# The first pair's turned rows made by TensorE products in a two-layer hybrid decoder with a mixture of experts

## What is computed

```python
def hier_moe(h, w_rg, b_rg, w_re, b_re, w_gate, w_up, w_down):
    xf = h.reshape(n_tok, d)                      # 512 tokens, d = 1024; h = rmsnorm(x)
    g_top = jnp.argmax(xf @ w_rg + b_rg)          # 1 of 4 groups
    chosen = (xf @ w_re + b_re)[of that group]    # 8 experts in it
    top_vals, top_idx = lax.top_k(chosen, 2)      # 2 experts a token
    weights = p_g[:, None] * jax.nn.softmax(top_vals, axis=-1)
    ...                                           # rows of a token are sent to its experts
    y = (jax.nn.silu(xc @ w_gate[e]) * (xc @ w_up[e])) @ w_down[e]
    ...                                           # weighted sum over a token's two experts
```

## Time and profile before

| what | value |
|---|---|
| median of three runs | 1655.12 us |
| profiled execution | 1655.6 us, of which the span is 1653.9 us |
| TensorE busy | 1560.3 us (94% of the span) |
| VectorE, ScalarE, GpSimd busy | 715.5, 308.2, 46.8 us |
| mean granted TensorE clock | 0.972 |
| DMA | 458 MB, mean 277 GB/s |

### The profile page before, as it was taken

The page is one execution under the profiler, slowest core; times in us unless marked ns, Lnnn a source line. Parts: engine busy times, 40 slices in busy tenths (PEclk is TensorE's granted clock), DMA queues, the critical chain, the costliest instruction groups (busy, mean ns, idle before and its releaser), DMA issues. The chain is left out here.

```text
span 1653.9 us, 19530 instructions
## 1 busy us (share of the span) xinstructions
PE 1560.3 (94%) x7428; PEld 730.9 (44%) x7428; DVE 715.5 (43%) x1550; ACT 308.2 (19%) x640; POOL 46.8 (3%) x62
## 2 busy tenths in 40 slices
PE   8999996999999999989999999997799999999995
PEld 4444452444443444445654444554344444444442
DVE  3222344334343333347265389824333333333335
ACT  2000120100000000022244277822000000000002
POOL 0000000000000000000000000000000000000000
PEclk9999997999999999999899899999899999999998
DMA  6271409999999999955210300072899999999993
GB/s 204 77 266 64 169 26 344 420 421 419 421 420 420 421 421 420 421 199 164 77 55 23 153 2 1 1 271 82 345 421 420 420 420 421 421 420 421 420 420 149
DMA packets 111931, 458.03 MB, mean 277 GB/s; under 512 B 29520, under 2 KB 56144, under 8 KB 62672
## 3 DMA queue, kind: packets, MB, share of 16 engines
q1 hardware_dynamic: 106352, 448.23, 67.5%
q0 software_dynamic: 5472, 8.40, 1.4%
HBM read 461.83 MB, written 6.29 MB: 283 GB/s over the span
## 5 line engine op out<-in xcount | busy, mean ns | idle before, releaser
L968 PE MATMUL ps<-raw,e_xT 128*64 128x512 f32 x2112 | 474.4, 600 | 16.8 <-DMA raw<-in_expert_w_up 16.8
L968 PEld LDWEIGHTS ps<-raw,e_xT 128*64 128x64 f32 x2112 | 154.7, 138 | 322.8 <-issue 321.5
L1105 DVE TENSOR_TENSOR e_sg_hid<-e_sg_hid,ps 64x512 f32<-64x512 f32 x66 | 45.0, 681 | 410.3 <-ACT e_sg_hid L1046 410.0
L1091 DVE TENSOR_TENSOR x_res<-x_res,ps 128x512 f32<-128x512 f32 x272 | 173.9, 681 | 4.3 <-PE ps L1006 2.1
L411 PE MATMUL ps<-c_hT,raw 128*128 128x512 f32 x384 | 165.2, 592 | 0.1
L996 PE MATMUL ps<-raw,e_hT 128*64 128x512 f32 x704 | 163.5, 607 | 1.3
L1054 ACT ACTIVATE e_yhi<-ps,e_wtab 128x512 fp32r<-128x512 f32 x66 | 45.3, 687 | 415.3 <-PE ps L996 415.3
L1046 ACT ACTIVATE e_sg_hid<-ps 64x512 f32<-64x512 f32 x66 | 39.2, 594 | 445.0 <-PE ps L968 445.0
L1777 PE MATMUL ps<-a_spare,raw 128*128 128x512 f32 x256 | 115.8, 609 | 3.8 <-DVE a_spare L1538 3.8
L1006 PE MATMUL ps<-e_yhi,e_pick 64*128 64x512 f32 x528 | 112.0, 421 | 6.5 <-DVE x_res L1091 4.8
L1084 DVE SCALAR_TENSOR_TENSOR e_ylo<-ps,e_wtab,e_yhi 128x512 fp32r<-128x512 f32 x66 | 49.6, 751 | 149.3 <-ACT e_yhi L1054 149.3
(11 more groups left out here) (289 smaller groups left out, 1357.7 us busy)
## 6 DMA issues: line engine op xcount, KB each, us to landing
raw<-in_expert_w_gate SPq DMA_DIRECT2D x128, 1024.0 KB, 25.6
raw<-in_expert_w_up SPq DMA_DIRECT2D x128, 1024.0 KB, 26.9
raw<-in_expert_w_down SPq DMA_DIRECT2D x88, 1024.0 KB, 27.0
e_raw<-in_expert_w_down SPq DMA_DIRECT2D x40, 1024.0 KB, 26.5
raw<-in_conv_w_in SPq DMA_DIRECT2D x11, 1024.0 KB, 9.7
raw<-in_w_kv SPq DMA_DIRECT2D x6, 1024.0 KB, 6.3
raw<-in_conv_w_out SPq DMA_DIRECT2D x1, 4096.0 KB, 19.0
raw<-in_attn_w_in SPq DMA_DIRECT2D x4, 1024.0 KB, 5.3
```

The lines of the kernel that those rows point to most:

```text
L968: mm = pe.matmul(ps_gu[C - C * i:2 * C - C * i, :], xT[:, q % 2, k, u * C:(u + 1) * C], ring(m, L, p)[:, kk * F:(kk + 1) * F], start=(k == ...
L1091: return dve.tensor_tensor(x, x, bank[:], ALU.add).then_inc(done, 1)
```

## The change

The gather of the first pair is gone. Instead, TensorE forms the turned rows of experts 0 and 1 directly: `x` of a token tile, every eighth column (`m.x[:, t, k:D:NK]`), is the operand loaded as weights, and the one-hot `first`, now float32 and scaled with the token's inverse norm (`rstd`), is the moving operand. There are 4 tiles times 8 groups of features, 32 products of 128x128 by 128x128, summed over the tiles in PSUM banks 4 and 2.

- The products of tiles 0 to 2 (24 of 32) stand before the last tile's choice: three before the last logits, 21 behind them. For them `rank` of tile 2 is made inside the last quarter and signalled (`s_ahead`), and VectorE makes the one-hots of those tiles (`first_pair(range(NT - 1))`, seven operations) between the last tile's two quarter additions. The other 8 products follow the last rank.
- The one-hot of one tile is two `tensor_scalar` operations of 128x64 with two per-partition factors, where one `tensor_tensor` of 128x512 made all four.
- `slots` moves out of the router's block into the experts' block (`vector_slots`), behind the scaling of the first pair.
- The place list (`vector_table`, `tensor_places`) moves behind chunk 0's down products, the indices, `vector_tail` and the table of weights to chunk 1; the table of weights stands in the middle of chunk 1's gate and up products. The second pair is turned in chunk 1, both halves, instead of one in chunk 0 and one in chunk 1.
- Pieces 8 to 11 are issued ahead of the last tile's `rows_x`, pieces 16 and 17 at the start of the experts' block without a wait, and the two `kv_scale` loads go to the end of the convolution.
- `m.code`, `idx0` and their operations are gone; several small tiles now lie in `coded`.

The loop on SyncE with the wait for `s_wt` is not touched.

```diff
@@ sync_ring
         for t in range(NT):
+            if t == NT - 1:
+                sp.wait_ge(self.s_o, 2 * NT + 1)
+                prefetch(sp, self.m, self.L, range(8, 12))
             sp.wait_ge(self.s_xn, t + 1)
             sp.dma_start(self.m.rows_x[self.L][t * P:(t + 1) * P, :], self.xn[:, t % 2, :]).then_inc(self.s_out[t % 2], 16)
-        sp.wait_ge(self.s_o, 2 * NT + 1)
-        prefetch(sp, self.m, self.L, range(8, 11))
@@ Router.tensor
+        def taken(tiles, ks):
+
+            for k in ks:
+                for t in tiles:
+                    mm = pe.matmul(m.ps[(4, 2)[k // HK]][:, k % HK * GS:(k % HK + 1) * GS], m.x[:, t, k:D:NK],
+                                   self.first[:, t, :], start=(t == 0 and k % HK == 0),
+                                   stop=(t == NT - 1 and k % HK == HK - 1))
+            return mm
...
+                    if part == 1 and k == 5:
+                        rank(t - 1).then_inc(self.s_ahead, 1)
...
         logits(NT - 1, 1, 0)
         turn(NT - 1, 1, 1)
+        pe.wait_ge(self.s_near, NT - 1)
+        pe.wait_ge(self.s_ev[0], NT)
+        taken(range(NT - 1), range(1))
         logits(NT - 1, 1, 1)
+        taken(range(NT - 1), range(1, NK))
         rank(NT - 1)
...
-        pe.wait_ge(self.s_near, 1)
-        for t in range(NT):
-            for i in range(2):
-                mm = pe.matmul(m.ps[2][:, 0:1], self.first[:, t, :], m.code[:, i, t:t + 1],
-                               start=(t == 0 and i == 0), stop=(t == NT - 1 and i == 1))
-        mm.then_inc(self.s_found, 1)
+        pe.wait_ge(self.s_near, NT)
+        for h in range(2):
+            taken(range(NT - 1, NT), range(h * HK, (h + 1) * HK)).then_inc(self.s_taken, 1)
@@ first_rows
-        pool.wait_ge(self.s_idx0, 1)
-        for s in self.s_out:
-            pool.wait_ge(s, 16 * (NT // 2))
-        self.gather(pool, 0, self.idx0[:])
@@ Router.vector
+        def first_pair(tiles):
+
             rank = m.ps[7][:, 0:NT * E].rearrange("p (t e) -> p t e", t=NT)
+            part = slice(tiles[0], tiles[-1] + 1)
+            own.step(dve.scalar_tensor_tensor(out=self.near[:, part], in0=rank[:, part, 0:PAIR], scalar=1.0,
+                                              in1=self.both[:, part, 0:PAIR], op0=ALU.add, op1=ALU.mult))
+            for t in tiles:
+                for e in range(PAIR):
+                    c = dve.tensor_scalar(self.first[:, t, e * C:(e + 1) * C], m.iota[:, 1:C + 1], self.near[:, t, e:e + 1],
+                                          m.rstd[:, self.n, t:t + 1], ALU.is_equal, ALU.mult)
+                c.then_inc(self.s_near, 1)
...
                 for part in range(2):
                     add(t, 1, part)
                     moved(t, part)
+                    if part == 0:
+                        dve.wait_ge(self.s_ahead, 1)
+                        first_pair(range(NT - 1))
...
         choose(NT - 1)
-        first_pair()
-        slots()
+        dve.tensor_tensor(self.w[:, 0, :], self.top[:, 1, :], self.top[:, 0, :], ALU.subtract).then_inc(self.s_ge, 1)
+        dve.wait_ge(self.s_rank, 1)
+        first_pair(range(NT - 1, NT))
@@ experts
-                if c == 0 and b == 0:
-                    r.tensor_places(pe)
+                if c == 1 and b == 0:
+                    pe.wait_ge(r.s_cw, 1)
+                    r.tensor_table(pe, ps_c[0][0], r.rhot[:].bitcast(F32), r.cwts[:], 2).then_inc(s_wt, 1)
...
             pe_transpose(pe, c)
-            if c + PAIR < NCH:
-                pe_turn(pe, c + PAIR)
+            for n in turns(c):
+                pe_turn(pe, n)
...
             pe_down(pe, c)
+            if c == 0:
+                r.tensor_places(pe)
...
-            sp.wait_ge(r.s_rows[0], 16)
-            prefetch(sp, m, L, (11, *range(NR0, NR)))
...
+            prefetch(sp, m, L, range(NR0, NR))
...
-            own = r.vector_table(dve)
-            r.vector_indices(dve, own)
-            r.vector_tail(dve, own)
+            own = r.vector_slots(dve)
...
-            for n in range(PAIR):
-                pe_turn(pe, n)
             for c in range(NB):
                 pe_step(pe, c)
```

More of the change, by code:

```diff
@@ L320, in _ @@
             r.sync_weights(sp)
+            with nc.allow_non_contiguous_dma(reason="small vectors"):
+                sp.dma_start(m.kv_scale[:, 0, :], a["norm_kv"].rearrange("(k p) -> p k", p=P)).then_inc(m.kv_gain, 16)
+                sp.dma_start(m.kv_scale[:, 1, :], a["norm_mix"][1].rearrange("(k p) -> p k", p=P)).then_inc(m.kv_gain, 16)
             prefetch(sp, m, 0, (6, 7, 12, 13, 14, 15))
@@ L490, in __init__ @@
         self.coded = sb(keep, "coded", [P, NTK * (C + 3 * NCH)])
+        marks = self.coded[:, 0:NTK * C].rearrange("p (w t e) -> p w t e", w=4, t=NT)
+        self.oh, self.slot, self.late = marks[:, 0:2], marks[:, 2], marks[:, 3]
+        self.first = self.coded[:, NTK * C:NTK * C + NT * GS].rearrange("p (t s) -> p t s", t=NT)
+        small = self.coded[:, NTK * (C + 2 * NCH):NTK * (C + 2 * NCH) + 8 * E].rearrange("p (w e) -> p w e", w=8)
+        self.zero, self.prior, self.hot, self.sel, self.cap, self.chunk, self.ovn, self.begin = (small[:, i] for i in range(8))
+        self.shift = self.coded[:, NTK * (C + 2 * NCH) + 8 * E:NTK * (C + 2 * NCH) + 8 * E + 2]
         self.idx, self.tok = sb(keep, "idx", [P, NCH // PAIR], U32), sb(keep, "tok", [P, NCH])
-        self.idx0 = sb(keep, "idx0", [P, 1], U32)
         self.rows = sb(keep, "rows", [P, 2, D])
@@ L495, in __init__ @@
         self.far = sb(keep, "far", [P, NCH])
-        self.near, self.first = sb(tmp, "near", [P, NT, PAIR]), sb(tmp, "first", [P, NT, GS], BF16)
+        self.near = sb(tmp, "near", [P, NT, PAIR])
         self.both = sb(tmp, "both", [P, NT, E], BF16)
@@ L755, in scaled_weights @@
             dve.wait_ge(self.s_wg, 1)
-        def first_pair():
-            dve.tensor_tensor(self.w[:, 0, :], self.top[:, 1, :], self.top[:, 0, :], ALU.subtract).then_inc(self.s_ge, 1)
-            dve.wait_ge(self.s_rank, 1)
-            rank = m.ps[7][:, 0:NT * E].rearrange("p (t e) -> p t e", t=NT)[:, :, 0:PAIR]
-            own.step(dve.scalar_tensor_tensor(out=self.near[:], in0=rank, scalar=1.0, in1=self.both[:, :, 0:PAIR],
-                                              op0=ALU.add, op1=ALU.mult))
-            dve.tensor_tensor(self.first[:].rearrange("p t (e c) -> p t e c", e=PAIR),
-                              m.iota[:, 1:C + 1].unsqueeze(1).unsqueeze(1).broadcast_to([P, NT, PAIR, C]),
-                              self.near[:].unsqueeze(3).broadcast_to([P, NT, PAIR, C]), ALU.is_equal).then_inc(self.s_near, 1)
-            dve.wait_ge(self.s_found, 1)
-            dve.tensor_scalar(self.idx0[:], m.ps[2][:, 0:1], FAR, None, ALU.add).then_inc(self.s_idx0, 1)
@@ L1049, in act_step @@
                 act.wait_ge(s_wtab, 1)
+                for s in r.s_out:
+                    act.wait_ge(s, 16 * (NT // 2))
             if NY <= c < E:
@@ L1072, in dve_turned @@
             q, h = n // 2, n % 2
-            wait(dve, s_xt, n + 1)
+            if n < PAIR:
+                dve.wait_ge(r.s_taken, n + 1)
+            else:
+                dve.wait_ge(s_xt, n - 1)
             wait(dve, s_used, (2 * q - 4) * NPIECE + 2 * NPIECE)
@@ L1216, in _ @@
             pool.wait_ge(r.s_idx, 2)
+            for s in r.s_out:
+                pool.wait_ge(s, 16 * (NT // 2))
             r.gather(pool, 1)
```

151 lines of the change are left out of this document (72 added, 79 removed).

## The result

The changed kernel is slower: 1661.93 us, median of 6 runs (1659.36 to 1663.53), against 1653.93 us (6 runs, 1650.1 to 1655.31) for the kernel before, measured beside it. The ratio is 1.005, 95% interval 1.004 to 1.006. The profiled execution took 1663.53 us, with a span of 1661.7; before, it was 1655.6. The forecast was 1645.0, range 1641 to 1659. The measured time is outside it, and within 1 us of the first rival's 1662.7.

What follows compares the result with a forecast made beforehand. The prediction took both layers' expert stages to end with the DMA's stream of weight pieces; -12.5 us (layer 0) and +1.2 (layer 1) on the profiled 1655.6 gave 1644.3, rounded to 1645, range 1641 to 1659.

Steps and rivals of the forecast that it cites:

- first rival: New products' weight loads run at ScalarE's strided pace, 0.54 us a product: 1662.7 us, slower; chance 0.22.
- the price with no row: Cost of new products loading x with a step of 8 floats: 0.222 us each taken, 0.54 the upper bound.
- Stages end with the stream of pieces: Both layers' expert stages end when the DMA's stream of weight pieces, at 420 GB/s, ends.
- One-hots 1.4 us: Last quarter, layer 0: VectorE makes three tiles' one-hots, near and six operations, in 1.4 us to 243.1.
- Rank at 250.3 and first gate product at 254.65: Layer 0: last rank delayed by 0.2 us only, first gate product at 254.65 instead of 261.77, 7.1 us earlier.
- Stream of layer 0: Layer 0's unbroken stream of pieces begins at 260.4 instead of 273.0: 12.6 us earlier, taken as 12.5.
- Stream of layer 1: Layer 1's stream starts at s_wt, 18.4 us after the first gate product, at 1176.1: 1.2 us later than before.
- Full clock behind the router: Behind the router TensorE's granted clock is 1.0 (2.4 GHz), where the mean was 0.76 from 260 to 280 us.
- Two chunks in 29 us: Experts' stage: chunks 0 and 1 take 29 us from first gate product, so layer 0's chunk 2 starts at 283.7.
- The second: Rival: weight loads about twice as long, 0.37 to 0.45 us a product, +8.6 to +13.2, 1653 to 1657.5; chance 0.18.
- The third: Rival: clock 0.5 in chunk 0 or late place chain, layer 1 losing 4 to 7 us, 1648 to 1651; chance 0.12.
- three signs that were to show me wrong: L579's instructions 0.2 us or more apart; layer 0's last SiLU moving under 8 us; layer 1's end not following gb.

Runs made afterwards that it cites:

- w_layout: Changed kernel with the first two experts' gate and up weights loaded in another row order, so products take 128 adjacent columns of x: 1646.52 us, ratio 0.9947.
- a_gb_late: Changed kernel with the gb load and its s_wt wait moved from chunk 2's to chunk 8's pieces in SyncE's queue: gained 13.7 us over the changed kernel.
- a_steps: Changed kernel with feature group k's new products loading x columns at a step of k+1 floats (1 to 8), first pair's rows wrong: 1676.28 us (one run).

## Why the prediction was wrong

**The step that failed is "the price with no row".** I bounded a product between 0.222 and 0.54 us and took the lower end, "since TensorE's load is the nearest kind of row". It was 0.480. With that price in my own formula, 58 x (0.480 - 0.222) = +15.0 us, the sum gives 1659.3 for a profiled 1663.5, slower and just past the point of 0.47 at which the first rival decides. `w_layout` is the counter-proof: with the price at 0.227 (42 instructions from 244.72 to 249.49) the same kernel takes 1646.52, where the sum had 1644.3. That ScalarE's pair of rows doubled with the same step was the better guide: it reads the same columns with the same step, and I had let the kind of instruction outweigh that.

**Point by point.**
- "Stages end with the stream of pieces": right. In all eleven kernels set against the one before, and in both layers, the ledger's microseconds and the shift of the last SiLU (the 33rd, where there are 34) agree within 2 us, over shifts from +8 to -23 us.
- One-hots 1.4 us: nearly right, `near` and six operations took 1.6 from 241.40. The last tile's addition came 0.79 us later (I had 0.93), the end of its choice only 0.5 (249.41 after 248.88).
- At 0.47 us a product I had written +14.6 us; my formula gives 14.4. It changes nothing.
- Rank at 250.3 and first gate product at 254.65: 255.55 and 262.18. In `w_layout` 249.57 and 253.99.
- Stream of layer 0, -12.5 us: with the true price my formula leaves -5.0; the last SiLU moved by -1.9. In `w_layout` it was -11.4.
- Stream of layer 1, `s_wt` 18.4 us after the first gate product: `gb` is issued 18.6 us after it (1162.68 to 1181.27). With the true price +8.7, measured 8.0 + 1.9 = 9.9.
- Both terms count twice, once in each layer: right.
- Full clock behind the router: wrong in layer 0. TensorE was granted 0.70 of it from 258 to 262 us and 0.50 from 262 to 266, and chunk 0's gate and up took 9.18 us. In `w_layout` the clock stayed at 1.00 there, and the same took 7.09. Why it fell in one and not in the other no run isolates. The timeline of the changed kernel and of `w_layout`, then the window in the same order:

```profile
262.18 9.18 PE L990 MATMUL ps<-raw,e_xT 128*64 128x512 f32 x32 [1.26 <-DVE e_xT L1102]
```
```profile
253.99 7.09 PE L994 MATMUL ps<-raw,e_xT 128*64 128x512 f32 x32 [1.26 <-DVE e_xT L1106]
```
```profile
262.00:266.00 4.00, 3.82 (x10) 1.24 (x12) 3.52 (x17) 0.60 (x1) 0.00 (x0) 0.50 0.93 338
```
```profile
262.00:266.00 4.00, 2.90 (x16) 1.34 (x18) 3.02 (x8) 0.00 (x0) 0.00 (x0) 1.00 1.02 430
```

- Two chunks in 29 us: wrong. From first gate product to chunk 2's was 35.8 us in layer 0 of the changed kernel, 31.1 in its layer 1, 32.0 in layer 0 of `w_layout`: 0.88 us for the scaling between the two turned halves, down products that ran partly at half clock, in the two stretches of layer 0 a wait for the gather, and in the first of the three also chunk 0 at half clock. `w_layout` has the slack for it; the changed kernel, in layer 0, has not.
- What was left of layer 0, 3.1 us, I put down to two places. One is chunk 0, above. The other is chunk 1: TensorE stood for the turned rows, the clock fell to 0.50, the down products took 6.20 us instead of 3.65, and the last window shown and the one behind it move 330 and 324 GB/s.

```profile
288.00:292.00 4.00, 2.07 (x14) 1.39 (x12) 1.12 (x2) 0.00 (x0) 0.00 (x0) 0.79 1.02 420
292.00:296.00 4.00, 4.00 (x11) 1.23 (x12) 1.48 (x3) 0.00 (x0) 1.20 (x1) 0.50 0.99 401
296.00:300.00 4.00, 4.00 (x18) 1.23 (x16) 0.75 (x1) 0.69 (x1) 0.00 (x0) 0.86 0.94 330
```

`a_gb_late`, whose layer 0 is the same program, had a clock of 0.69 and 0.88 in the first two of these windows and ended the layer 2.0 us sooner; its chunk 0 was as slow (8.86 us). So the part in chunk 1 varies from one execution to the next, and I have no kernel that isolates either: the split is argued, not shown.

**Rivals.** The first is what happened: the loads are slow by their step, and the kernel with them. Its cause is another than ScalarE's pace of one element in 2.10 ns: a doubling that is complete at a step of four. That its 1662.7 is within 1 us of the time is partly luck: it had +18.4 us for a price of 0.54, the measured price gives 15.0, and the rest, 3.1 us in layer 0 and 1.2 in layer 1, it did not count. The second had the right size of the load, about twice, and stopped at 0.45 a product. The third came in part: half clock in chunk 0, and chunk 1 late, in layer 0. But it put its loss in layer 1 by a late `s_wt`, and there `gb` came 18.6 us behind the first gate product, as in the sum. Of the three signs that were to show me wrong two stood in the profile: L579 was 0.240 apart, and layer 0's last SiLU moved by less than 8 us. The third did not come: layer 1's end did follow `gb`.

## What to carry to other kernels

Before an operand is read with a step, ask how many of its elements share 16 bytes: here float32 weight loads kept their pace at two in 16 bytes and took twice the time at one, however far the step beyond that, up to the eight tried. In a kernel that is fed by a ring, count the bytes moved up to a fixed time behind the stage's start: that number turned into microseconds told the stage's end within 2 us in every kernel here, while an earlier load, a busier TensorE and a higher mean clock did not. And look for the wait that stands in the middle of the queue: the small `gb` load stood before the ring's refill in layer 1, and moving it was worth 13.7 us in the changed kernel, nearly what the step cost; in the kernel before the same edit was worth nothing, so ask first what the freed pieces will run beside.

## What the runs showed of the hardware that I had not expected

- A 128x128 float32 weight load at full clock (2.4 GHz) began 0.11 us behind the one before at a step of one float, 0.12 at two, 0.17 at three and 0.22 to 0.24 at four to eight (`a_steps`).
- The second pair's gather beside the stream of 1 MB pieces lands later: 3.3 us after its issue with the queue standing (52 GB/s), 8.1 with the stream running (417 GB/s), in layer 1 of the changed kernel and of `a_gb_late`.
- Not of the hardware, but as unexpected: an edit that changes values changes the work: one more chunk, 16.7 us, in the next layer, which hid a gain of 15 us entirely. The count of SiLU rows showed it at once.
